# One step for the scores of both maps of a prompt query block, with matmuls alternating between the two row halves

## The reference

```
h = rms_norm(x);  u = h @ w_in            # [1152, 1024] x [1024, 6144]
branch A (differential attention, 4 heads, two maps of 64 dims each):
    s[m] = q[m] . k[m] / 8                # m = 0, 1
    w = softmax(mask(s[0])) - lam * softmax(mask(s[1]));   o = w @ v      # v has 128 dims
branch B (stick-breaking attention, 8 heads of 64 dims):
    z = q . k / 8
    a = exp(log_sigmoid(z) + reverse cumulative sum of log_sigmoid(-z));  o = a @ v
x = x + (gate_a * (norm(o_A) * silu @ w_a) + gate_b * (o_B * silu @ w_b)) @ w_out
```

## Time and profile before

| What | Value |
|---|---|
| Median of three runs | 3462.72 us |
| Profiled execution, own time | 3463.09 us |
| Span of the profiled execution | 3461.3 us |
| Busy share TensorE / VectorE / ScalarE | 89% / 46% / 26% |
| Mean granted clock of TensorE | 0.864 of full speed |
| One head of phase_attention (start of its first scores to the next head's) | 133.12 us, eight of them in the program |
| Matmuls of L810 | 768 records, 443.0 us busy |

### The profile page before, as it was taken

One profiled execution on the slowest core, in us unless ns is written; L12 is line 12 of the kernel. 1 busy time (PEld: TensorE's weight loads), 2 busy tenths in 40 slices (PEclk: granted clock), 3 DMA queues, 4 the chain that ended last, 5 costly groups with the idle time before them and its releaser, 6 DMA issues. The chain is left out here.

```text
span 3461.3 us, 52533 instructions
## 1 busy us (share of the span) xinstructions
PE 3097.3 (89%) x21296; PEld 2299.0 (66%) x21296; DVE 1591.5 (46%) x1999; ACT 895.7 (26%) x1537; POOL 0.2 (0%) x4
## 2 busy tenths in 40 slices
PE   4989999999899999879868999999998999997895
PEld 3767677776666656658656767767765666665684
DVE  3634344444154554564356333444432554654553
ACT  2212222222142332320031222222222332333101
POOL 0000000000000000000000000000000000000000
PEclk9999999999876676689989999999997775775898
DMA  6378786676201100054344778767742010012444
GB/s 216 110 242 292 259 296 212 226 239 207 90 28 38 31 28 25 19 202 133 113 148 163 260 260 281 258 221 247 235 154 74 27 46 23 27 28 89 153 145 158
DMA packets 315425, 519.46 MB, mean 150 GB/s; under 512 B 40224, under 2 KB 111008, under 8 KB 315168
## 3 DMA queue, kind: packets, MB, share of 16 engines
q1 hardware_dynamic: 315248, 516.89, 44.4%
HBM read 436.58 MB, written 84.93 MB: 151 GB/s over the span
## 5 line engine op out<-in xcount | busy, mean ns | idle before, releaser
L335 PE MATMUL A_acc<-A_w_hi,A_ht_hi 128*128 128x512 f32 x1728 | 721.5, 418 | 38.1 <-DVE A_w_lo L540 19.1
L335 PE MATMUL A_acc<-A_w_lo,A_ht_hi 128*128 128x512 f32 x1728 | 684.9, 396 | 0.0
L335 PE MATMUL A_acc<-A_w_hi,A_ht_lo 128*128 128x512 f32 x1728 | 683.9, 396 | 0.0
L810 PE MATMUL B_sc<-B_kt,B_qt 64*128 64x512 f32 (+3 forms) x768 | 443.0, 697 | 16.9 <-DVE B_kt L891 15.5
L335 PEld LDWEIGHTS A_acc<-A_w_hi,A_ht_hi 128*128 128x128 f32 x1728 | 331.1, 192 | 134.1 <-issue 26.8
L335 PEld LDWEIGHTS A_acc<-A_w_hi,A_ht_lo 128*128 128x128 f32 x1728 | 330.7, 191 | 74.2
L335 PEld LDWEIGHTS A_acc<-A_w_lo,A_ht_hi 128*128 128x128 f32 x1728 | 332.1, 192 | 57.7
L831 PE MATMUL B_ov<-B_nat_v,B_wt 128*128 128x64 f32 (+1 forms) x1728 | 322.9, 362 | 14.4 <-DVE B_wt L891 14.4
L555 DVE STREAM_TRANSPOSE A_kt<-A_kt 128x2048 f32<-128x2048 f32 x128 | 293.1, 2302 | 76.5 <-DMA A_kt<-in_cache_da_k 69.5
L831 PEld LDWEIGHTS B_ov<-B_nat_v,B_wt 128*128 128x128 f32 x1728 | 305.8, 272 | 20.8 <-issue 20.8
L810 PEld LDWEIGHTS B_sc<-B_kt,B_qt 64*128 64x128 f32 x768 | 163.9, 245 | 156.0 <-issue 137.5
(11 more groups left out here) (132 smaller groups left out, 3287.6 us busy)
## 6 DMA issues: line engine op xcount, KB each, us to landing
A_kt<-in_cache_da_k SPq DMA_DIRECT2D x64, 1024.0 KB, 10.8
A_v<-in_cache_da_v SPq DMA_DIRECT2D x64, 1024.0 KB, 5.8
A_kt<-in_cache_sb_k SPq DMA_DIRECT2D x64, 1024.0 KB, 11.4
A_v<-in_cache_sb_v SPq DMA_DIRECT2D x64, 1024.0 KB, 5.8
A_w_raw<-in_w_in SPq DMA_DIRECT2D x96, 512.0 KB, 4.6
tmp_gates<-A_stage SPq DMA_DIRECT2D x72, 256.0 KB, 4.3
D_gate<-tmp_gates SPq DMA_DIRECT2D x72, 256.0 KB, 3.5
D_w_raw<-in_w_merge SPq DMA_DIRECT2D x32, 512.0 KB, 6.1
```

Source lines behind the costliest of these rows:

```text
L335: last = nc.tensor.matmul(acc[:, n % 2, :], h[:, k, rows], w[:, slot, cols], start=(k == 0 and j == 0), stop=(k == KC - 1 and j == 2))
L810: nc.tensor.matmul(sc[:, m, c:e], qkt[0][m * HD:(m + 1) * HD, qb * P:(qb + 1) * P], qkt[1][m * HD:(m + 1) * HD, c:e], start=True, stop=(e ...
```

## The change

The two score steps of an item become one. TensorE waits once, until the functions of both maps of the item before are done; then it issues, for each piece of 512 keys, the matmul of map 0 on rows 0 to 63 and that of map 1 on rows 64 to 127; then the two mask matmuls, one after the other. In `attention_steps` the two "max" steps now follow the joint scores step, and the two "functions" steps follow these. The number of instructions of each kind does not change.

```diff
--- before.py
+++ after.py
@@ -641,26 +641,27 @@
     def slice_in(a):
         return [(rounds, "slice_t", a, which, half) for which in range(2) for half in range(2)]
 
-    def scores(n, m):
-        add("scores", n, m)
+    def scores(n):
+        add("scores", n)
         if n < NP_T:
-            add("max", n, m)
+            for m in range(2):
+                add("max", n, m)
 
     def values(n):
         add("values", n)
         add("out", n)
 
     merged(slice_in(0))
+    scores(0)
     for m in range(2):
-        scores(0, m)
         add("functions", 0, m)
     for n in range(ITEMS):
         if n == NP_T - 1:
             merged(slice_in(1))
         add("weights", n)
         if n + 1 < ITEMS:
+            scores(n + 1)
             for m in range(2):
-                scores(n + 1, m)
                 add("functions", n + 1, m)
         if n:
             values(n - 1)
@@ -746,13 +747,13 @@
                 def body(h, last):
                     for step in STEPS:
                         kind = step[0]
-                        if kind == "scores" and step[1:] == (0, 0):
+                        if kind == "scores" and step[1] == 0:
 
                             turned(sp, h, last_slice[0])
                             load_queries_keys(h, 1)
                             sp.wait_ge(S["pv_done"], h * ITEMS)
                             load_slice(h, nat_v[1], dram["v_sb"][l], v_nat_sems[1])
-                        elif kind == "scores" and step[1:] == (NP_T, 0) and not last:
+                        elif kind == "scores" and step[1] == NP_T and not last:
                             turned(sp, h, last_slice[1])
                             load_queries_keys(h + 1, 0)
                         elif kind == "out":
@@ -798,18 +799,20 @@
                                 pe.wait_ge(S["nat_q" if which == 0 else "nat_k"], h * 32 + 16 * (a + 1))
                             transpose_round(r, [nat[which][:, half * 4 + j, :] for j in range(4)])
                         elif kind == "scores":
-                            _, n, m = step
+                            n = step[1]
                             a, qb = n // NP_T, n % NP_T
                             keys = (qb + 1) * P
-                            if (qb, m) == (0, 0):
+                            if qb == 0:
                                 copied(pe, h, last_slice[a])
 
-                            pe.wait_ge(S["s_free"], h * (2 * ITEMS) + (2 * n + m - 1))
+                            pe.wait_ge(S["s_free"], h * (2 * ITEMS) + 2 * n)
                             for c in range(0, keys, BLK):
                                 e = min(keys, c + BLK)
-                                nc.tensor.matmul(sc[:, m, c:e], qkt[0][m * HD:(m + 1) * HD, qb * P:(qb + 1) * P],
-                                                 qkt[1][m * HD:(m + 1) * HD, c:e], start=True, stop=(e < keys))
-                            nc.tensor.matmul(sc[:, m, qb * P:keys], ident_r, mask_r[a], start=False, stop=True).then_inc(S["qk_done"], 1)
+                                for m in range(2):
+                                    nc.tensor.matmul(sc[:, m, c:e], qkt[0][m * HD:(m + 1) * HD, qb * P:(qb + 1) * P],
+                                                     qkt[1][m * HD:(m + 1) * HD, c:e], start=True, stop=(e < keys))
+                            for m in range(2):
+                                nc.tensor.matmul(sc[:, m, qb * P:keys], ident_r, mask_r[a], start=False, stop=True).then_inc(S["qk_done"], 1)
                         elif kind == "prob_t":
                             _, n, u, j, r = step
                             if j == 0:
```

## The result

| | before | after |
|---|---|---|
| Median of four runs | 3459.51 us | 3259.15 us (3247.99 to 3276.17) |
| Profiled execution, own time / span | 3463.09 / 3461.3 us | 3276.17 / 3274.4 us |
| Third head, scores to scores | 133.12 us | 109.18 us |

The ratio is 0.9427, 95% interval 0.9379 to 0.9475: faster by 5.7%. The forecast was 3341 us with a range from 3265; the time lies 6 us under the range. The sign was right, the size was not. The profiled execution, from which all rows and the table by items are read, was the longest of the four.

The account below looks back on a forecast made before the run. TensorE was taken to bound a head to first order (busy 126.1 of 133.12 us). Savings of 7.1 + 1.6 + 6.5 = 15.2 us per head, 122 us for eight heads, gave 3341 us; 8-in-10 range 3265 to 3400.

Parts of the forecast that it names:

- Row halves overlap: Score matmuls on TensorE: full overlap, both maps in the time of one; second weight load counted at 0.1 us.
- Rival three: Score matmuls: the pair is staggered by one pass, about 5.5 us per head back, 3385 us; chance 0.06.
- The second mask costs 0.40: Score step: the second mask matmul adds 0.40 us to the first, bounded by 0.1 and 0.40.
- The joint wait and the late minima set the pace of branch A: Items 0 to 7: scores wait for both maps' exponentials, minima start late; sum 49.7 to 42.6, 7.1 us less per head.
- the terms given for it, 6.5 and 3.5: Item 7: ScalarE's copy comes 6.5 us after the start, then 3.5 of slices; length forecast 11.0 to 10.3 us.
- Items 8 to 13 gain 1.6 us: Branch B, full clock: VectorE and ScalarE chain without scores; 1.6 us gained in items 10 to 12, bounds 0 and 5.6.
- The tail after item 15's scores has no scores in it and keeps its time: End of each head, values and transposes after item 15's scores: no time saved.
- items 14 and 15 "half clock": Items 14 and 15, TensorE-bound at half clock: one map's passes go, 3.1 + 3.4 = 6.5 us per head.
- Rival one: Granted clock moves up in items 3 to 5, 14 and 15: some 5 us more per head, 3300 us; chance 0.24.
- with parts of the tail too, 3260: Clock-up case extended: parts of the tail after item 15's scores also at full clock, 3260 us.
- Rival two: Clock moves down: items 6 and 7 stay at 0.50, 3378 us; items 8 to 13 too, 3458; chance 0.14.

Follow-up runs that it names:

- experiment 1: Against the changed kernel: all score blocks of map 0 issued before those of map 1, instead of alternating; 3255.1 us, ratio 0.9429.
- first run with fillers: Eight unused matmuls per head behind scores of items 0 to 2, against the changed kernel with ScalarE's copies before map 1's sigmoids; 3193.5 us, ratio 0.9263.
- Experiments 2 and 3: Against the changed kernel: each map's mask right behind its matmuls, so no overlap, 3627.6 us; every pair of score matmuls issued twice, 3345.8 us.
- the serial kernel: Changed kernel with the joint wait, but each map's mask right behind its own matmuls, so halves cannot overlap; 3627.6 us, ratio 1.0504.

## Why the prediction was wrong

- *Row halves overlap.* Right, fully: in the trace's records of item 5 two passes start at 1170.335 and 1170.341 us and the next two at 1170.868 and 1170.875, and eight take the time of four. The records do not name the map; since a map's two passes ran one behind the other before, I read each pair as one pass of either map. Rival three wanted a whole pass between the maps. The Trainium skill (TensorE: Matmul & The Clock Gate, Part 3: matmuls start and end in program order) does not hold here: in experiment 1 map 1's passes of 512 columns start (by 1159.856) before those of 256 columns of map 0 (1160.272), which stand ahead of them in the program.
- *The second mask costs 0.40.* Too high: in item 4, at the half clock, it starts 0.27 us behind the first (records at 1167.251 and 1167.522), in item 5, at the full clock, 0.17 (1171.826 and 1171.991).
- *The joint wait and the late minima set the pace of branch A.* Right in place and size: items 2, 3, 6 and 7 came to 3.97, 4.75, 5.34 and 10.31 (forecast 4.0, 4.75, 5.55, 10.3), with the idle time in front of L812 put down to L875. Item 7's 10.3 is in part luck: the terms given for it, 6.5 and 3.5, add up to 10.0, the slices did begin 6.5 us after its scores, and where it runs at 1.00 in other heads it takes 9.85. Item 1, which was to grow from 2.9 to 3.6, took 2.53 here and 2.80 in the mean of eight heads.
- *Items 8 to 13 gain 1.6 us.* Wrong: they came out 0.1 longer in this head and 1.0 in the mean of eight. Their chain is as read, with TensorE's wait for ScalarE's copy now 2.39 where it was 1.59; item 8 is 1.7 longer, at a clock of 0.57 behind 1.99 us of idle time. In the first run with fillers item 7 and item 8 ran at 1.00 and item 8 took 3.84, its old length.
- *"The tail after item 15's scores has no scores in it and keeps its time", and items 14 and 15 "half clock".* This is the step that failed. I priced every item at the clock that it had before. Items 5, 14 and 15 with the tail ran at 1.00, 0.83 and 0.68, and took 1.8, 2.7 and 4.2 us less than forecast, together the 8.7 by which the third head beat its sum; eight times that is 70 of the 82 us between forecast and median. Of the 4.2, 2.5 lie in item 15's score step (2.2 us to the first values, where 8.1 less 3.4 was forecast) and 1.8 behind it, without any change in the instructions there. The rest of the head's differences cancel.
- *Rival one* had this mechanism, at 5 us per head and a chance of 0.24, and "with parts of the tail too, 3260". It was the case that came, though its hit on 3259 is partly luck: it had 3.3 us per head from items 3 to 5, of which item 3 gave nothing (it stayed at 0.50), item 4 0.3 and item 5 1.8, and the larger part came from item 14 and from item 15 with the tail. The stated range began at 3265, above this rival's own 3260. Its ground, that full-height work ran just ahead of the rise while long half-height scores did not raise the clock, was in the trace, and should have weighed more than a forecast with frozen clocks. Experiments 2 and 3 show for the head as a whole that it is the halves at work, not the shorter step: same step lengths, 0.60 against 0.84. For the tail they do not show it, since there the serial kernel gained too.
- *Rival two* was the weaker: item 7 (0.90) and item 8 (0.57) did lose clock, some 2 us per head.

What stays open: why heads of one trace, and two profiles of one kernel, differ in an item's clock (item 2 with fillers: 1.00 and 0.56), and what moved the clock of the tail. The 220 us of experiments 2 and 3 are an estimate from the mask's price in three items.

## What to carry to other kernels

Matmuls on different row halves into different banks run side by side in fp32 even when whole groups stand between them in the program, as long as no full-height matmul does. When an edit changes what TensorE has at work, price it at both clocks: here about a third of the gain (8.7 of 24 us in the third head, by my sum) came as clock, part of it in steps that were not touched. Once the passes are halved the chain through the other engines is the bound, so look next at the order of the copies (50 us here) and at a spare half of the score buffer (30 us).

## What the runs showed of the hardware that I had not expected

- Full-height matmuls of no use, in an 11 us stretch with idle time of TensorE, shortened it by 2.0 us in the best heads (clock 0.55 to 1.00) and raised its clock in 10 heads of 16.
- The same passes without overlap, with only the wait made joint, cost 5.0%; 1.6% was foreseen.
- A second full-height mask matmul starts 0.17 us behind a first at the full clock and 0.27 at the half, where the matmul of one row half behind a mask started 0.26 and 0.40 us after it.
- Map 1's passes overtook a matmul of map 0 that stands ahead of them in the program (experiment 1, item 5).
